# A transformer block pair on one core: the first two units behind three norms multiplied jointly, roundings freed of squares, convolution steps interleaved, unread matmuls in TensorE's gaps

## What is computed

```
h    = rmsnorm(x, norm_mix_pre);  proj = h @ w_in
xr   = rg_lru(causal_depthwise_conv(xr));  y_rnn = xr * gelu(yr)
mix  = sigmoid(g_rnn) * (y_rnn @ w_rnn_proj) + sigmoid(g_attn) * (attention @ w_attn_proj)
x    = x + rmsnorm(mix @ w_out, norm_mix_post)
h    = rmsnorm(x, norm_mlp_pre)
x    = x + rmsnorm(square(relu(h @ w_mlp_up)) @ w_mlp_down, norm_mlp_post)
h    = rmsnorm_2(x, norm_attn_2)      # second block: three kinds of attention,
x    = x + heads @ w_out_2            # then a gated MLP with a short convolution
out  = rmsnorm_2(x + conv_ffn(rmsnorm_2(x, norm_mlp_2)), norm_final_2)
```

## Time and profile before

| | |
|---|---|
| median of 3 runs | 2847.97 us (2847.93 to 2851.32) |
| the profiled execution | 2851.61 us |
| its span, first to last instruction | 2849.8 us |
| busy: PE, PE weight loads, VectorE, ACT, POOL | 2759.1, 2402.6, 1957.4, 1328.6, 108.1 us |
| mean granted TensorE clock | 0.989 |
| DMA | 503.31 MB, mean 177 GB/s |
| chain that ended last | PE 82%, VectorE 8%, issue 5%, ACT 3% |

### The profile page before, as it was taken

One profiled execution on the slowest core, in us unless ns is written; L12 is line 12 of the kernel. 1 busy time (PEld: TensorE's weight loads), 2 busy tenths in 40 slices (PEclk: granted clock), 3 DMA queues, 4 the chain that ended last, 5 costly groups with the idle time before them and its releaser, 6 DMA issues.

```text
span 2849.8 us, 50569 instructions
## 1 busy us (share of the span) xinstructions
PE 2759.1 (97%) x16378; PEld 2402.6 (84%) x16378; DVE 1957.4 (69%) x3071; ACT 1328.6 (47%) x2115; POOL 108.1 (4%) x203
## 2 busy tenths in 40 slices
PE   5999999999998999999999899999999999999998
PEld 4888888888886888888888689788888888888887
DVE  6777867766757775457754664765788885688855
ACT  4565555554444444334443443554554444444443
POOL 0000000000010000000000010100010000000000
PEclk9999999999999999999999999999999999999999
DMA  4444544445553556556655444444445545555554
GB/s 155 176 164 173 192 159 156 147 166 187 182 193 117 185 183 221 207 200 216 203 201 197 148 171 158 148 166 145 160 163 191 188 172 192 194 185 189 182 172 162
DMA packets 83499, 503.31 MB, mean 177 GB/s; under 512 B 9813, under 2 KB 18293, under 8 KB 31819
## 3 DMA queue, kind: packets, MB, share of 16 engines
q1 hardware_dynamic: 79868, 491.04, 49.2%
q0 software_dynamic: 2992, 10.86, 1.4%
q10 hardware_dynamic: 576, 0.58, 0.1%
HBM read 500.29 MB, written 10.55 MB: 179 GB/s over the span
## 4 chain that ended last, share of the span: by engine, by line
PE 82%; DVE 8%; issue 5%; ACT 3%; DVEq 1%; ACTq 0%; DMA 0%
PE PS L555 47%; PE PS L561 24%; ACT w L1066 2%; DVE w L1610 2%; DVE tmp L1621 1%; PE PS L637 1%; PE PS L638 1%; PE PS L639 1%; PE PS L572 1%; PE PS L574 1%; PE PS L573 1%; DVE tmp L2001 0%; DVE tmp L2000 0%; PE PS L812 0%; PE PS L660 0%
## 5 line engine op out<-in xcount | busy, mean ns | idle before, releaser
L1610 DVE TENSOR_TENSOR w<-w_raw,w 128x1024 fp32r<-128x1024 f32 (+1 forms) x964 | 1098.5, 1173 | 410.4 <-ACT w L1066 409.1
L1066 ACT ACTIVATE w<-w_raw 128x1024 fp32r<-128x1024 f32 (+1 forms) x964 | 939.8, 1010 | 399.3 <-PE PS L561 238.1
L555 PE MATMUL PS<-h,w 128*128 128x512 f32 x3104 | 807.3, 401 | 19.0 <-DVE h L1644 10.5
L555 PEld LDWEIGHTS PS<-h,w 128*128 128x128 f32 x3104 | 562.1, 190 | 151.1 <-issue 27.9
L561 PEld LDWEIGHTS PS<-h,w 128*128 128x128 f32 x3104 | 425.0, 191 | 31.0
L555 PE MATMUL PS<-u,w 128*128 128x512 f32 x1728 | 443.0, 395 | 5.2 <-ACT w L1066 5.2
L561 PE MATMUL PS<-h,w 128*128 128x256 f32 x3104 | 434.1, 283 | 0.0
L555 PEld LDWEIGHTS PS<-u,w 128*128 128x128 f32 x1728 | 309.6, 190 | 58.6 <-ACT w L1066 5.8
L555 PE MATMUL PS<-f,w 128*128 128x512 f32 x1408 | 354.4, 394 | 4.0 <-DVE x L2236 4.0
L555 PEld LDWEIGHTS PS<-f,w 128*128 128x128 f32 x1408 | 254.2, 190 | 49.8 <-DVE x L2236 4.2
L561 PEld LDWEIGHTS PS<-u,w 128*128 128x128 f32 x1728 | 241.9, 191 | 21.1
(11 more groups left out here) (308 smaller groups left out, 2434.8 us busy)
## 6 DMA issues: line engine op xcount, KB each, us to landing
w_raw<-in_w_FU SPq DMA_DIRECT2D x88, 1024.0 KB, 4.7
w_raw<-in_w_UP SPq DMA_DIRECT2D x64, 1024.0 KB, 4.8
w_raw<-in_w_DN SPq DMA_DIRECT2D x64, 1024.0 KB, 4.7
w_raw<-in_w_FD SPq DMA_DIRECT2D x64, 704.0 KB, 4.1
w_raw<-in_w_G SPq DMA_DIRECT2D x32, 1024.0 KB, 4.7
w_raw<-in_w_Q SPq DMA_DIRECT2D x18, 1024.0 KB, 4.7
w_raw<-in_w_X SPq DMA_DIRECT2D x16, 1024.0 KB, 4.8
w_raw<-in_w_Y SPq DMA_DIRECT2D x16, 1024.0 KB, 4.7
```

Of the source, the lines that this page charges most:

```text
L555: pe.matmul(PS[:, bank, :], w_hi[:, 2 * s + hf, k * P:(k + 1) * P], rhs[:, k0 + k].rearrange("p a b -> p (a b)"), start=start and k == 0, ...
L1066: act.activation(w_hi[:, 2 * s + hf, 0:n * P], w_raw[:, s, off * P:(off + n) * P], ACT.Copy)\
L1610: tt(w_lo[:, slot, 0:n * P], w_raw[:, s, off * P:(off + n) * P], w_hi[:, slot, 0:n * P].bitcast(F32), ALU.subtract).then_inc(lo_ready, 1)
```

## The change

- **Joint first pair.** For X, UP0 and C2 a new `first_pair` does units 0 and 1 together: for each chunk of h the wide matmul of both units, banks 0 and 1, so each chunk is used twice as it arrives. After eight chunks come the narrow matmuls of both first halves; in the second half the narrow ones follow each wide one. `half_done` is raised by 1 after the first half and by 3 at the end. The weights of unit 1 are split ahead of the chunks, those of unit 2 in two parts around the root.
- **Unread matmuls.** `keep_busy(n, a, b)` issues n fp32r matmuls of 512 columns into PSUM bank 6, which nobody reads: 10 before X, 4 within each of `sum_features(1)` and `(3)`, 3 after each of three table matmuls, 16 and 12 around norm 4's squares.
- **Norm 0.** ACT squares four chunks by one instruction into a tile of its own, `x_sq`, as x lands, VectorE adds them in wide steps. Only par is loaded by ACT (own semaphore `par_landed`); const, pos and sinks are issued by POOL once x has landed and waited for at RG's rope tables and before Q. The exponential of lambda moves behind the roundings.
- **Gains and rounding.** `normalise` multiplies two chunks at once by the reciprocal, without the gain; ACT's rounding and VectorE's low part apply the gain. In the branches ACT multiplies the gain into O's and DN1's output during those products (`branch_gain`), and VectorE scales and adds two chunks at once. In `squares_and_hi` both roundings of a pair come before its squares.
- **X's convolution.** VectorE merges first, and the two low halves (now for the unit two ahead) stand between the taps; a tap's wait on the one before is placed behind the instruction in between (`link.mark`, `link.wait`). ACT rounds xr first, then the weights.

The diff, cut to its core (TensorE's and POOL's part, then ACT's, then VectorE's):

```diff
+            pool.wait_ge(x_landed[3], 16)
+            pool.dma_start(const[:], dram["const"]).then_inc(small_landed, 16)
+            pool.dma_start(pos_i[:], dram["pos"].partition_broadcast(P)).then_inc(small_landed, 16)
+            pool.dma_start(sinks[:], dram["sinks"].partition_broadcast(P)).then_inc(small_landed, 16)
...
+            def first_pair(name, rhs, ready, norm):
+                u, pair = U0[name], [(0, 0), (1, 1)]
+                pe.wait_ge(acc_free, T0[name] + 2)
+                def follow(k):
+                    if norm is not None:
+                        add_square(norm, k)
+                    pe.wait_ge(ready[0], ready[1] + k + 1)
+                def high(s, hf, k):
+                    c = HALF * hf + k
+                    pe.matmul(PS[:, s, :], w_hi[:, 2 * s + hf, k * P:(k + 1) * P], rhs[:, c].rearrange("p a b -> p (a b)"),
+                              start=c == 0, stop=False)
+                def low_part(s, hf, k):
+                    c = HALF * hf + k
+                    return pe.matmul(PS[:, s, S:2 * S], w_lo[:, 2 * s + hf, k * P:(k + 1) * P], rhs[:, c, 0, :],
+                                     start=False, stop=c == NC_D - 1)
+                pe.wait_ge(hi_ready, 2 * u + 3)
+                for k in range(HALF):
+                    follow(k)
+                    for s in range(2):
+                        high(s, 0, k)
+                pe.wait_ge(lo_ready, 4 + 2 * u + 3)
+                for s in range(2):
+                    for k in range(HALF):
+                        mm = low_part(s, 0, k)
+                mm.then_inc(half_done, 1)
+                pe.wait_ge(hi_ready, 2 * u + 4)
+                pe.wait_ge(lo_ready, 4 + 2 * u + 4)
+                for k in range(HALF):
+                    follow(HALF + k)
+                    for s in range(2):
+                        high(s, 1, k)
+                        mm = low_part(s, 1, k)
+                mm.then_inc(half_done, 3)
...
+                if joint:
+                    first_pair(name, rhs, ready, norm)
+                elif peel or ready:
...
+                if norm == 1:
+                    keep_busy(4, d_hi[:, 0, 0:P], d2[:, 0].rearrange("p a b -> p (a b)"))
+                elif norm == 3:
+                    keep_busy(4, u_hi[:, 0, 0:P], u2[:, 0].rearrange("p a b -> p (a b)"))
...
+            def keep_busy(n, a, b):
+                for _ in range(n):
+                    pe.matmul(PS[:, 6, :], a, b, start=True, stop=True)
             sum_features(0)
-            product("X", 16, h2, ready=(h_ready, 4))
+            pe.wait_ge(hi_ready, 1)
+            keep_busy(10, w_hi[:, 0, 0:P], w_hi[:, 0, 0:2 * S])
+            product("X", 16, h2, ready=(h_ready, 4), joint=True)
...
+                if var < 3:
+                    keep_busy(3, d_hi[:, 0, 0:P], d2[:, 0].rearrange("p a b -> p (a b)"))
...
+            keep_busy(16, u_hi[:, 0, 0:P], u2[:, 0].rearrange("p a b -> p (a b)"))
...
+            keep_busy(12, u_hi[:, 0, 0:P], u2[:, 0].rearrange("p a b -> p (a b)"))
...
+            def squares_and_hi(gain):
+                for i in range(NC_D // 2):
+                    act.wait_ge(x_new, n_x[0] + 2 * i + 2)
+                    for c in (2 * i, 2 * i + 1):
+                        act.activation(h_hi[:, c, :], x[:, c, :], ACT.Identity, scale=pcol(gain, c)).then_inc(h_hi_ready, 1)
+                    for c in (2 * i, 2 * i + 1):
+                        act.wait_ge(ss_step, n_sq[0] + c + 1)
+                        act.activation(tmp[c % 2][:, 0:S], x[:, c, :], ACT.Square).then_inc(sq_ready, 1)
+                n_sq[0] += NC_D
+                n_x[0] += NC_D
+            def branch_square(c, s):
+                act.wait_ge(ss_step, n_sq[0] + c + 1)
+                act.activation(tmp[s][:, 0:S], qy[:, c, :], ACT.Square).then_inc(sq_ready, 1)
+            def branch_gain(gain, c):
+                act.activation(qy[:, c, :], qy[:, c, :], ACT.Identity, scale=pcol(gain, c)).then_inc(gain_scaled, 1)
...
+            for k in range(4):
+                act.wait_ge(x_landed[k], 16)
+                own = slice(4 * k, 4 * k + 4)
+                act.activation(x_sq[:, own, :], x[:, own, :], ACT.Square).then_inc(sq_ready, 4)
+            n_sq[0] += NC_D
+            unit_hi(0, 0, SUB)
+            deviation()
+            unit_hi(0, 1, SUB)
+            act.wait_ge(par_landed, 16)
+            round_h("norm_mix_pre")
...
+            def body(i, first=False, last=False):
                 for s in range(2):
                     c, pair = 2 * i + s, U0["X"] // 2 + i
-                    next_hi(pair, s, n)
-                    if not isinstance(i, int) or i + s:
+                    if not first or s:
                         conv_hi(c - 1)
+                    if not last or s == 0:
+                        half_hi(pair + 1, s, 0, SUB)
                     act.wait_ge(acc_free, 2 + T0["X"] + c + 1)
                     act.wait_ge(xr_ready, c + 1)
                     act.activation(tmp[2 + s][:, 0:S], tmp[s][:, 3:3 + S], ACT.Identity, scale=pcol("conv_w", 4 * c + 3),
                                    bias=pcol("conv_b", c)).then_inc(tap_ready, 1)
-            run_pairs(act, "X", 8, body, peel=True)
+                    if not last or s == 0:
+                        half_hi(pair + 1, s, 1, SUB)
...
+                        elif s == 0:
+                            next_hi(U0[name] // 2, 1, n, 0)
                             deviation()
+                            next_hi(U0[name] // 2, 1, n, 1)
...
+            dve.wait_ge(sq_ready, 8)
+            link(tt(x_sq[:, 0:4, :], x_sq[:, 0:4, :], x_sq[:, 4:8, :], ALU.add))
+            dve.wait_ge(sq_ready, 12)
+            link(tt(x_sq[:, 0:4, :], x_sq[:, 0:4, :], x_sq[:, 8:12, :], ALU.add))
+            link(tt(x_sq[:, 0:2, :], x_sq[:, 0:2, :], x_sq[:, 2:4, :], ALU.add))
+            dve.wait_ge(sq_ready, 16)
+            link(tt(x_sq[:, 12:14, :], x_sq[:, 12:14, :], x_sq[:, 14:16, :], ALU.add))
+            link(tt(x_sq[:, 0:2, :], x_sq[:, 0:2, :], x_sq[:, 12:14, :], ALU.add))
+            tt(sq_sum[:], x_sq[:, 0, :], x_sq[:, 1, :], ALU.add).then_inc(ss_step, NC_D)
...
+            def normalise(gain, mid=None):
                 inverse_deviation()
-                bufs = [tmp[k][:, 0:S] for k in (4, 5, 0, 1)]
-                def scaled(c, s):
-                    dve.wait_ge(h_ready, n_h[0] + c + 1)
-                    stt(bufs[s], x[:, c, :], pcol(gain, c), rstd, ALU.mult, ALU.mult).then_inc(hv_ready, 1)
-                def lo(c, s):
-                    dve.wait_ge(h_hi_ready, n_h[0] + c + 1)
-                    tt(h_lo[:, c, :], bufs[s], h_hi[:, c, :].bitcast(F32), ALU.subtract).then_inc(h_ready, 1)
+                bufs = [4, 0]
+                def scaled(p, b):
+                    dve.wait_ge(h_ready, n_h[0] + 2 * p + 2)
+                    tt(windows(tmp[bufs[b]], 0, P, 0, [[264, 2], [1, S]]), x[:, bass.ds(2 * p, 2), :], rstd_twice, ALU.mult)\
+                        .then_inc(hv_ready, 2)
+                def lo(p, b):
+                    for s in range(2):
+                        c = 2 * p + s
+                        dve.wait_ge(h_hi_ready, n_h[0] + c + 1)
+                        stt(h_lo[:, c, :], tmp[bufs[b] + s][:, 0:S], pcol(gain, c), h_hi[:, c, :].bitcast(F32),
+                            ALU.mult, ALU.subtract).then_inc(h_ready, 1)
                 scaled(0, 0)
                 scaled(1, 1)
-                if with_first_unit:
-                    half_lo(0, 0, 0, SUB)
-                    half_lo(0, 0, 1, SUB)
-                with dve.Fori(0, NC_D // 4 - 1) as i:
-                    for s in range(4):
-                        scaled(4 * i + s + 2, (s + 2) % 4)
-                        lo(4 * i + s, s)
-                for c in range(NC_D - 4, NC_D):
-                    if c + 2 < NC_D:
-                        scaled(c + 2, (c + 2) % 4)
-                    lo(c, c % 4)
+                lo(0, 0)
+                scaled(2, 0)
+                lo(1, 1)
+                if mid:
+                    mid()
+                with dve.Fori(1, 3) as i:
+                    for b in range(2):
+                        scaled(2 * i + b + 1, 1 - b)
+                        lo(2 * i + b, b)
+                scaled(7, 1)
+                lo(6, 0)
+                lo(7, 1)
...
+                def scaled(p):
+                    dve.wait_ge(gain_scaled, n_b[0] + 2 * p + 2)
+                    own = bass.ds(2 * p, 2)
+                    tt(qy[:, own, :], qy[:, own, :], rstd_twice, ALU.mult).then_inc(branch_scaled, 2)
+                def add(p):
+                    dve.wait_ge(branch_scaled, n_b[0] + 2 * p + 2)
+                    own = bass.ds(2 * p, 2)
+                    tt(x[:, own, :], x[:, own, :], qy[:, own, :], ALU.add).then_inc(x_new, 2)
+                def lo(p):
+                    for s in range(2):
+                        if next_gain:
+                            gain_lo(2 * p + s, h_lo, h_hi, next_gain)
                 scaled(0)
```

(58 more changed lines are left out.)

172 lines of the change are left out of this document (90 added, 82 removed).

## The result

The changed kernel took 2828.4 us (median of 4 runs, 2827.4 to 2830.5), the kernel before 2848.9 beside it; the ratio is 0.9928 (95% interval 0.9911 to 0.9945): 20.5 us faster. The profiled execution took 2830.5 (span 2828.7), 21.1 less than the one before.

The account below looks back on a forecast made before the run. PE, busy 97% of the span, was taken as the bound, so only its idle or half-rate stretches could give time. Terms of -9.7 (start to Q), -6.6 and -4.4 summed to -20.7 us: 2827.3 for the median, range 2817 to 2840.

Parts of the forecast that it names:

- Start: Up to the end of X's first pair: squares stop waiting for small loads; pair ends at 36.8, against 49.64: -12.8 us.
- The hole: In X's first pair: PE has nothing to do behind chunk 3, from about 20.7 to 25.1, some 4 us.
- X's loop: VectorE starts a unit behind, cycle 5.6 us, last merge at 120.5: +3.35; stall before RG grows to some 5 us.
- RG: From X's last merge to Q: one low part less in the way in the new last step, -0.25 us.
- A slow start of PE is hidden: In RG: its end is set by VectorE's queue, so a slow PE start costs nothing, before or after.
- O to UP0: Behind O: joint pair with the clock up; UP0's loop starts at 900.1, against 906.7: -6.6 us.
- DN1 to C2: Behind DN1: faster squares, hidden fillers, joint pair ending at 1645.2 against 1650.34, less 0.7 for a merge: -4.4 us.
- R2: X and start: VectorE's cycle 5.3 shortens the stall before RG, -4 more; x landing at 9, -1; 2822 us, chance 0.13.
- R3: Loops swallow the gain: UP0 gives 2 in place of 6.6, X 3 less; 2835 us, chance 0.14.
- R4: X's loop: w_raw is freed late; with loads landing at 12.2 the cycle is 8.35, costing 38 us; 2865, chance 0.03.
- R1: Clock stays down, second halves of the pairs double: X +6, UP0 +4, C2 +4; 2841 us, chance 0.15.

Follow-up runs that it names:

- loads_first: The changed kernel with the three small loads issued by ACT at the start, nothing of the start waiting for them: 2829.8 us.
- wait_all: The changed kernel with the three small loads issued by ACT first and ACT's squares waiting for all four loads again: 2836.7 us in one run.
- swap_hi: The changed kernel with two ACT steps exchanged in X's loop, the first half of the weight rounding ahead of the rounding of xr: 2826.8 us.
- serial_loop: The changed kernel with the convolution's steps in X's loop one after the other again, both low halves last: 2832.5 us.
- hole8: The changed kernel with eight more unread matmuls in X's first pair, between chunks 3 and 4: 2829.9 us in one run.
- combo_a: The changed kernel with ACT's exchange, even pairs in UP0 and C2, eight matmuls in X's first pair, one filler instead of three between table matmuls: 2829.3 us.

## Why the prediction was right

It gave 2827.3 (2817 to 2840), faster with 0.92; 2828.4 came. By its own steps, against 20.7 forecast and 21.1 measured in the profiled executions:

- **Start, -12.8.** Measured -13.2: the last narrow matmul of the pair ends at 36.47. x's last part landed at 9.3 (I took 10.0), but VectorE was the bound then and made four adds, not three; the terms that I wrote for the ones-matmul give 14.0, not 14.4, and it ended at 14.45. The weights landed at 11.7 (13.6): in loads_first ACT takes them at 13.46, so putting the small loads behind x brought them 1.7 earlier, which I had excluded; the root did not wait for them. The hole (3.6, "from about 20.7 to 25.1") is as written. The wait was the cost, as loads_first and wait_all show.
- **X's loop, +3.35.** The term that failed most: measured +0.8 (the last merge starts 81.16 behind the pair's end, 80.35 before). The cycle is 5.46, not 5.6: its links are those I wrote (xr, ACT's rounding of it, the weight's, low half, taps, low half), but they sum to the lower part of my 5.2 to 5.8. VectorE waits for the weight's rounding, which stands behind that of xr, as in this row of the changed kernel's timeline:

```profile
103.08 1.23 DVE L1705 TENSOR_TENSOR w<-w_raw,w 128x1024 fp32r<-128x1024 f32 x1 [1.01 <-ACT w L1128]
```

swap_hi shows that the rounding of xr is what closes the cycle; serial_loop puts 5.70 back. The stall before RG was 3.0, not 5.
- **RG, -0.25.** Measured -0.93 from merge to Q. The first pair of low halves comes 5.95 behind the merge (6.32 before), without the short waits between taps, and VectorE's wait of 0.59 for ACT's next rounding is gone. "A slow start of PE is hidden" is borne out: Q is 29.8 behind the merge in five runs with a slow start of RG, and in the changed kernel's with a fast one.
- **O to UP0, -6.6.** Measured -5.2. The first chunk is on PE 9.2 behind O, not 8.1: the first square's matmul stands 8.8 behind O, 7.9 without fillers, so they hold it up 0.9, not 0.4. The nine between the table's matmuls lengthen that piece by some 2.8 (6.6 in place of 3.8), more than nine times 0.23; that the changes between the two kinds of matmul cost the rest is my reading, no run separates it. A pair of chunks takes 2.4, not 2.1: VectorE waits 0.25 for ACT's roundings. The clock did stay at 1.0. PE's third unit comes 7.2 earlier behind O (28.95 against 36.14), and 1.8 of it go by the start of the fourth unit, 1.48 of them as PE's wait for that unit's weights (888.06 above; I had 2.2). ACT's rounding for it, 40.6 behind O before (905.65), is 35.2 behind it now, as the timeline of ACT shows:

```profile
886.96 1.99 ACT L1128 ACTIVATE w<-w_raw 128x1024 fp32r<-128x1024 f32 x2
```

That is 5.4 earlier, and the loop gave it on. Joint pair and fillers make up 3.9 and 0.2 of the 5.2; the rest is left to gains and joint adds, which no run takes out.
- **DN1 to C2, -4.4.** Measured -2.8. The first chunk comes only 0.4 earlier behind DN1 (22.35 against 22.74), where I had 0.9 at the root already. The chunks come 0.81 apart, not 0.74, and the wide matmuls ran at half rate, which the forecast didn't have here. The table of stretches of the changed kernel:

```profile
1612.00:1616.00 4.00, 1.98 (x9) 1.03 (x7) 3.69 (x8) 2.06 (x5) 0.00 (x0) 1.00 1.05 418
1616.00:1620.00 4.00, 4.00 (x11) 2.99 (x12) 3.55 (x8) 2.37 (x6) 0.00 (x0) 0.57 0.61 254
1620.00:1624.00 4.00, 4.00 (x29) 3.69 (x28) 3.75 (x9) 1.98 (x5) 0.00 (x0) 1.00 0.00 0
```

The fillers end 1.7 before the first chunk, and the clock falls to 0.57 behind it. They were not just hidden; they gave 2 us. Taken out one at a time, the joint pair (3.2) and the fillers (2.1) cost more than the whole 2.8 here, so the joint scalings and gains gave nothing in C2 or the two parts overlap; no run separates this.

So the total was right because two misses cancel: the start, X and RG gave 3.6 more (2.5 + 0.7 + 0.4), UP0 and C2 3.0 less. That the total came within 1.1 us is luck: each of the five has its sign right, but three are off by 1.4 to 2.5. R2's mechanism (a shorter cycle) came true in half its size, R3's in UP0 not at all. R4 would have needed w_raw to land late; in X's loop VectorE waits for ACT alone. R1 did not come: the second halves of all three pairs ran at full rate, even without fillers, so no run measures its 14 us.

## What to carry to other kernels

When the consumer of a hand-over is late, work on the producer's queue decides how much of a gain upstream arrives: here PE's 1.6 us in X came to nothing until one rounding of ACT stood in front of another. Put fillers in front of the wait, not behind it, and only where the stretch behind it is not hidden; check each one against the stage's own distance, since the whole scatters by as much as it gives. Ask of each edit what the stage as a whole gained: X's part of this one gave nothing behind its first ones-matmul. And look for a wait that covers more than its reader needs: one such wait, for three loads that nobody read for 100 us, was worth 7 us, the largest single part.

## What the runs showed of the hardware

- Short waits of PE do not always cost the clock. A wait of 3.0 to 3.1 ahead of RG was followed by a low rate in six experiments and by the full one in two traces (the changed kernel and hole8). Behind the one of 2.2 in serial_loop the full rate lasted 1.1 us, then came the low one. A wait of 1.3 ahead of RG was never followed by it (four runs), but in three of these the clock fell at a wait of 1.76 later. The wait of 1.84 or 1.85 at Q was followed by a fall in the changed kernel, hole8, combo_a and the kernel before, and by none in eight others. Each fall cost 1.5 us where PE is the bound.
- At the start matmuls ran at half rate (0.43 per 512 columns, fillers among them, for 4.8 us) while the view of clocks gives 1.00; the first mean below 1.00 is given for 24 to 28 us.
- The part behind C2, the same code in all fourteen traces, took 1195.0 to 1200.7 us.
